# Last layer norm of tile 1's front half: moments turned into two rows and added by a rank-2 product, with GpSimd weighting by g and finishing one piece of tile 0

## The reference

```python
def layer_norm(x, g, b):
    xf = x.astype(jnp.float32)
    mu = jnp.mean(xf, axis=-1, keepdims=True)
    var = jnp.mean(jnp.square(xf - mu), axis=-1, keepdims=True)
    y = (xf - mu) * lax.rsqrt(var + LN_EPS) * g.astype(jnp.float32) + b.astype(jnp.float32)
    return y.astype(x.dtype)
...
        x = layer_norm(DEEPNORM_ALPHA * x + attn_out, ln1_g[l], ln1_b[l])
        hdn = jnp.square(jax.nn.relu(jnp.einsum('bsd,df->bsf', x, w_ff1[l])))
        ff_out = jnp.einsum('bsf,fd->bsd', hdn, w_ff2[l])
        x = layer_norm(DEEPNORM_ALPHA * x + ff_out, ln2_g[l], ln2_b[l])
```

## Time and profile before

| | |
|---|---|
| median of 3 runs | 1088.48 us (1087.71 to 1088.55) |
| the profiled execution | 1088.89 us, its span 1087.1 us |
| PE busy | 1081.4 us (99%) |
| DVE busy | 822.6 us (76%) |
| ACT busy | 578.2 us (53%) |
| POOL busy | 24.5 us (2%), 43 instructions |

### The profile page before, as it was taken

How to read it: one execution, slowest core, us unless ns; L and a number is a source line. 1 busy time by engine, 2 the same in 40 slices (tenths; PEclk the granted TensorE clock), 3 DMA queues, 4 the chain that set the end, 5 groups by cost and what they waited for, 6 DMA issues and landing times.

```text
span 1087.1 us, 13951 instructions
## 1 busy us (share of the span) xinstructions
PE 1081.4 (99%) x5586; PEld 918.4 (84%) x5586; DVE 822.6 (76%) x923; ACT 578.2 (53%) x756; POOL 24.5 (2%) x43
## 2 busy tenths in 40 slices
PE   9999999999999999999999999999999999999998
PEld 7888888888888888888888888888888888888886
DVE  6587758666666685667699999766776678889998
ACT  6487757665544524445465456444454455545461
POOL 1000101010000000000000000000000000000000
PEclk9999999999999999999999999999999999999999
DMA  9857665557545835665656566566656655655862
GB/s 300 263 177 224 185 191 156 175 177 247 176 155 168 285 108 156 192 193 176 218 189 231 169 220 232 167 188 191 191 174 204 219 177 198 228 195 190 282 222 78
DMA packets 108048, 213.84 MB, mean 197 GB/s; under 512 B 6784, under 2 KB 38016, under 8 KB 107472
## 3 DMA queue, kind: packets, MB, share of 16 engines
q1 hardware_dynamic: 107216, 209.61, 60.1%
q0 software_dynamic: 624, 3.21, 1.0%
q10 hardware_dynamic: 144, 0.13, 0.0%
HBM read 210.83 MB, written 2.10 MB: 196 GB/s over the span
## 4 chain that ended last, share of the span: by engine, by line
PE 98%; DVE 1%; DMA 1%; issue 0%; SPq 0%; ACT 0%; DVEq 0%
PE low_ps L802 11%; PE low_ps L639 10%; PE high_ps L802 9%; PE high_ps L824 7%; PE high_ps L823 7%; PE high_ps L822 7%; PE low_ps L531 6%; PE low_ps L527 6%; PE low_ps L529 6%; PE low_ps L808 5%; PE high_ps L808 5%; PE low_ps L644 5%; PE low_ps L823 3%; PE low_ps L824 3%; PE low_ps L822 3%; PE high_ps L576 1%
## 5 line engine op out<-in xcount | busy, mean ns | idle before, releaser
L1333 DVE TENSOR_TENSOR w_lo<-w_raw,w_hi 128x1024 fp32r<-128x1024 f32 x175 | 213.1, 1222 | 133.6 <-ACT w_hi L993 132.2
L993 ACT ACTIVATE w_hi<-w_raw 128x1024 fp32r<-128x1024 f32 x175 | 185.1, 1059 | 188.5 <-PE low_ps L531 69.5
L802 PE MATMUL low_ps<-x1T,w_hi 128*128 128x512 f32 x512 | 177.3, 393 | 0.0
L802 PE MATMUL high_ps<-x1T,w_hi 128*128 128x512 f32 x448 | 155.1, 393 | 0.0
L639 PE MATMUL low_ps<-xT,w_hi 128*128 128x512 f32 x448 | 144.2, 398 | 0.0
L808 PE MATMUL low_ps<-x1T,w_lo 128*128 128x256 f32 x512 | 139.3, 278 | 0.0
L1663 DVE TENSOR_TENSOR w_lo<-w_raw,w_hi 128x1024 fp32r<-128x1024 f32 x72 | 87.0, 1222 | 59.7 <-ACT w_hi L1194 59.7
L1218 ACT ACTIVATE sum_hi<-sum_raw 128x1024 fp32r<-128x1024 f32 x60 | 63.6, 1063 | 124.7 <-DVE sum_raw L1685 112.8
L808 PE MATMUL high_ps<-x1T,w_lo 128*128 128x256 f32 x448 | 122.1, 278 | 0.0
L1194 ACT ACTIVATE w_hi<-w_raw 128x1024 fp32r<-128x1024 f32 x72 | 76.1, 1060 | 86.4 <-PE low_ps L802 43.4
L802 PEld LDWEIGHTS low_ps<-x1T,w_hi 128*128 128x128 f32 x512 | 94.9, 187 | 20.1
(11 more groups left out here) (214 smaller groups left out, 1915.4 us busy)
## 6 DMA issues: line engine op xcount, KB each, us to landing
w_raw<-in_w_ff SPq DMA_DIRECT2D x208, 512.0 KB, 4.3
w_raw<-in_w_in SPq DMA_DIRECT2D x93, 512.0 KB, 4.3
more_raw<-in_w_ff SPq DMA_DIRECT2D x42, 512.0 KB, 5.2
w_raw<-in_w_out SPq DMA_DIRECT2D x32, 512.0 KB, 3.7
x_raw<-in_x_turned SPq DMA_DIRECT2D x8, 256.0 KB, 6.4
y<-in_x SPq DMA_DIRECT2D x8, 256.0 KB, 4.6
side_raw<-in_w_ff SPq DMA_DIRECT2D x4, 512.0 KB, 6.7
w_raw<-in_w_in SPq DMA_DIRECT2D x6, 256.0 KB, 5.8
```

Source lines behind the costliest of these rows:

```text
L802: return pe.matmul(banks[:, b, :], w_hi[:, slot, cols], x1T[:, t, :, :].rearrange("p h t -> p (h t)"), start=(t == 0 and not lows_open), s ...
L993: act.activation(w_hi[:, slot, :], w_raw[:, slot, :], ACT.Copy).then_inc(w_rounded, units)
L1333: dve.tensor_tensor(w_lo[:, slot, :], w_raw[:, slot, :], w_hi[:, slot, :].bitcast(F32), ALU.subtract).then_inc(w_split, units)
```

## The change

The moments of tile 1 no longer go through DVE's `centre` for its first half. With d the standard deviation and s = 1/d, the norm is written s(gy - mg + db). POOL multiplies the first half of tile 1 by g as soon as its four statistics are taken. PE brings this gy into PSUM through the identity. Once the moments are known, ACT takes the root d; PE turns the two columns (m, d) of 128 tokens into two rows of 128; ACT copies these out, with the sign of m flipped (`row_signs`); and PE adds for each piece one product of these two rows with two rows that hold g and b (`gb_rows`, loaded from HBM by two new DMAs of 4 KB). ACT's copy out of PSUM now multiplies by s. DVE's two `centre` instructions on this half are gone, and its four last instructions are two `centre` and two `finish_norm`.

Piece 2 of tile 0 leaves PE and ACT: POOL multiplies it by s and adds b, in two instructions. POOL thus runs three instructions on 1024, 512 and 512 columns that it didn't have. ACT runs one Sqrt ahead of the norm, and loads a table for it. DVE sets three small constants at the start. SP stores piece 3 ahead of piece 7.

```diff
 SCALED = [3, 4, 5, 6]
-COPIED = [2] + SCALED
-STORE_ORDER = [0, 1, 2, 7, 3, 4, 5, 8]
+FIRST_HALF = slice(0, HALF)
+BY_POOL = 2
+STORE_ORDER = [0, 1, BY_POOL, 3, 7, 4, 5, 8]
...
+                    sp.dma_start(gb_rows[n:n + 1, :], v[:, FIRST_HALF]).then_inc(rows_loaded, 16)
...
-        pe.wait_ge(tail_summed, 2)
-        pe.wait_ge(gb2_loaded, 32)
-        pe.matmul(high_ps[:, 1, :], ident_t[:, :], ln2_gb[:, 1, LAST_PIECES[2][1]], start=True, stop=False)
-        pe.wait_ge(diag_ready, 1)
-        pe.wait_ge(centred, len(PIECES) + 3)
-        pe.matmul(high_ps[:, 1, :], diag[0][:, :], y1[:, 0, LAST_PIECES[2][1]], start=False,
-                  stop=True).then_inc(y2_scaled, 1)
         pe.wait_ge(low_drained, 4)
+        pe.wait_ge(weighted, 1)
         for i in SCALED:
-            pe.matmul(scaled_ps(i), ident_t[:, :], ln2_gb[:, 1, LAST_PIECES[i][1]], start=True,
-                      stop=False)
-        pe.wait_ge(diag_ready, TT)
-        for n, i in enumerate(SCALED):
-            tt, cols = LAST_PIECES[i]
-            pe.wait_ge(centred, len(PIECES) + (6 if i > 4 else 4))
-            pe.matmul(scaled_ps(i), diag[1][:, :], y1[:, tt, cols], start=False,
+            pe.matmul(scaled_ps(i), ident_t[:, :], y1[:, 1, LAST_PIECES[i][1]], start=True, stop=False)
+        pe.wait_ge(tail_summed, 3)
+        pe.wait_ge(moments, 2 * TT)
+        pe.wait_ge(mean_std_ready, 1)
+        pe.matmul(high_ps[0:2, 2, 0:P], mean_std, ident_t[:, :], start=True, stop=True).then_inc(
+            moments_turned, 1)
+        pe.wait_ge(rows_loaded, 32)
+        pe.wait_ge(rows_ready, 1)
+        for i in SCALED:
+            pe.matmul(scaled_ps(i), moment_rows[0:2, :], gb_rows[0:2, LAST_PIECES[i][1]], start=False,
                       stop=True).then_inc(y2_scaled, 1)
...
-        def finish_piece(i, centred_before):
-            finish_norm(1, count + centred_before, 1, LAST_PIECES[i][1], y1, ln2_gb, y2_ready)
-
-        centre(1, 1, slice(0, 512), y1, ln2_gb)
         centre(1, 1, LAST_PIECES[7][1], y1, ln2_gb)
-        finish_piece(7, 5)
-        centre(1, 1, slice(512, 1024), y1, ln2_gb)
         centre(1, 1, LAST_PIECES[8][1], y1, ln2_gb)
-        finish_piece(8, 7)
+        finish_norm(1, count + 4, 1, LAST_PIECES[7][1], y1, ln2_gb, y2_ready)
+        finish_norm(1, count + 5, 1, LAST_PIECES[8][1], y1, ln2_gb, y2_ready)
...
+        pool.wait_ge(gb2_loaded, 32)
+        pool.wait_ge(y2_stats, 4)
+        pool.tensor_tensor(y1[:, 1, FIRST_HALF], y1[:, 1, FIRST_HALF], ln2_gb[:, 0, FIRST_HALF],
+                           ALU.mult).then_inc(weighted, 1)
+        inverse_std(1, 0)
+        front = y1[:, 0, LAST_PIECES[BY_POOL][1]]
+        pool.wait_ge(centred, len(PIECES) + 3)
+        pool.wait_ge(std_ready, TT + 1)
+        pool.tensor_scalar(front, front, inv_std[:, 0:1], None, ALU.mult).then_inc(front_scaled, 1)
+        pool.wait_ge(front_scaled, 1)
+        pool.tensor_tensor(front, front, ln2_gb[:, 1, LAST_PIECES[BY_POOL][1]], ALU.add).then_inc(
+            front_ready, 1)
+        inverse_std(1, 1)
```

More of the change, by code:

```diff
@@ L175, in hybrid_layer @@
     mid = at("mid", [P, 2 * TT, NC], F32, 48 * KB)
-    diag = [at(f"diag{tt}", [P, P], F32, 48 * KB + 512 * tt) for tt in range(TT)]
+    moment_rows = at("moment_rows", [P, P], F32, 48 * KB)
     X0 = 56 * KB
@@ L221, in hybrid_layer @@
     last_raw = at("last_raw", [P, 4 * NC], F32, H0 + 24 * KB)
+    gb_rows = at("gb_rows", [P, HALF], F32, X0 + 28 * KB)
     own_hi = [at("own_hi0", [P, 3 * NC], F32R, H0 + 77 * KB), at("own_hi1", [P, 3 * NC], F32R, X0)]
@@ L244, in hybrid_layer @@
     eps_sum = part(42, 2)
+    last_std, eps_one, row_signs = part(40, 1), part(44, 1), part(45, 1)
+    mean_std = small[:, 34:41:6]
     stats = part(48, TT * CHUNKS * 6 + 6)
@@ L313, in hybrid_layer @@
     y2_stats, y2_ready, stored = sem("y2_stats"), sem("y2_ready"), sem("stored")
-    diag_ready, y2_scaled, y2_copied = sem("diag_ready"), sem("y2_scaled"), sem("y2_copied")
+    rows_loaded, mean_std_ready, moments_turned = sem("rows_loaded"), sem("mean_std_ready"), sem("moments_turned")
+    rows_ready, y2_scaled, y2_copied = sem("rows_ready"), sem("y2_scaled"), sem("y2_copied")
+    weighted, front_scaled, front_ready = sem("weighted"), sem("front_scaled"), sem("front_ready")
     x_d = x.rearrange("b (t p) d -> p (b t) d", p=P)
@@ L452, in sync_program @@
             tt, cols = LAST_PIECES[i]
-            if i in COPIED:
-                sp.wait_ge(y2_copied, COPIED.index(i) + 1)
+            if i in SCALED:
+                sp.wait_ge(y2_copied, SCALED.index(i) + 1)
+            elif i == BY_POOL:
+                sp.wait_ge(front_ready, 1)
             else:
-                sp.wait_ge(y2_ready, i + 1 - len([n for n in COPIED if n < i]))
+                sp.wait_ge(y2_ready, [0, 1, 7, 8].index(i) + 1)
             sp.dma_start(out_d[:, tt, cols], y1[:, tt, cols]).then_inc(stored, 16)
@@ L1304, in scalar_program @@
         copy_first(3)
[L1306 to L1316, removed]
+        act.wait_ge(powers_ready, 5)
+        act.activation(last_std, eps_one, ACT.Sqrt)
+        act.wait_ge(moments, TT + 1)
+        act.activation(var_eps[:, 0:1], mean_var[:, 1:2], ACT.Copy, bias=EPS).then_inc(var_ready, 1)
+        act.wait_ge(moments, TT + 2)
+        act.activation(last_std, mean_var[:, 3:4], ACT.Sqrt, bias=eps_one).then_inc(mean_std_ready, 1)
+        act.activation(var_eps[:, 1:2], mean_var[:, 3:4], ACT.Copy, bias=EPS).then_inc(var_ready, 1)
+        act.wait_ge(moments_turned, 1)
+        act.activation(moment_rows[0:2, :], high_ps[0:2, 2, 0:P], ACT.Copy, scale=row_signs[0:2, :]).then_inc(
+            rows_ready, 1)
+        act.wait_ge(std_ready, 2 * TT)
         for n, i in enumerate(SCALED):
             tt, cols = LAST_PIECES[i]
-            act.wait_ge(y2_scaled, n + 2)
-            act.activation(y1[:, tt, cols], low_ps[:, n, 0:cols.stop - cols.start],
-                           ACT.Copy).then_inc(y2_copied, 1)
+            act.wait_ge(y2_scaled, n + 1)
+            act.activation(y1[:, tt, cols], low_ps[:, n, 0:cols.stop - cols.start], ACT.Copy,
+                           scale=inv_std[:, 1:2]).then_inc(y2_copied, 1)
         for i in BY_SCALAR:
             tt, cols = LAST_PIECES[i]
-            act.wait_ge(y2_copied, SCALED.index(i) + 2)
+            act.wait_ge(y2_copied, SCALED.index(i) + 1)
             act.dma_start(out_d[:, tt, cols], y1[:, tt, cols]).then_inc(stored, 16)
@@ L1449, in vector_program @@
         dve.memset(eps_sum, HEAD_DIM * EPS).then_inc(powers_ready, 1)
+        dve.memset(eps_one, EPS).then_inc(powers_ready, 1)
+        dve.memset(row_signs, 1.0).then_inc(powers_ready, 1)
+        dve.wait_ge(powers_ready, 4)
+        dve.memset(row_signs[0:1, :], -1.0).then_inc(powers_ready, 1)
         def split_opening(u):
@@ L1919, in rms_scale, with inverse_std, first_scale @@
             pool.tensor_tensor(o_scale, root, inv_sums[h % 3][:, 0:4:2], ALU.mult).then_inc(scale_ready, 1)
[L1921 to L1931, removed]
+        def inverse_std(norm, tt):
+            n = TT * norm + tt + 1
+            pool.wait_ge(var_ready, n)
+            pool.tensor_tensor(inv_std[:, tt:tt + 1], var_eps[:, tt:tt + 1],
+                               minus_half[:, tt:tt + 1], ALU.pow).then_inc(std_ready, 1)
+        def first_scale(tt):
+            pool.wait_ge(moments, tt + 1)
+            pool.tensor_scalar(var_eps[:, tt:tt + 1], mean_var[:, 2 * tt + 1:2 * tt + 2], EPS,
+                               None, ALU.add).then_inc(var_ready, 1)
+            inverse_std(0, tt)
         pool.wait_ge(w_used, SLOTS + 1)
@@ L1947, in gpsimd_program @@
                 "p l d -> p (l d)")).then_inc(gb1_loaded, 16)
-        norm_scale(0)
-        norm_scale(1)
+        for tt in range(TT):
+            first_scale(tt)
+        pool.wait_ge(gb2_loaded, 32)
[11 more added lines that the diff above has]
+        inverse_std(1, 1)
     with nc.Block() as block:
```

## The result

The changed kernel took 1090.8 us (median of 13 runs, 1089.98 to 1091.3), the kernel before 1088.28 in the same series (1087.71 to 1089.05). The ratio is 1.0022, with a 95% interval of 1.0015 to 1.0029: 2.4 us slower, between 1.6 and 3.2. The prediction was 1090.4, in a range of 1088.0 to 1091.2.

The account below looks back on a forecast made before the run. PE fills 98% of the chain, but DVE leads without a gap up to tile 1's moments. Terms 1.3 + 0.9 - 0.3 = +1.9 us, on the median of 1088.48, gave 1090.4 us, range 1088.0 to 1091.2.

Parts of the forecast that it names:

- What bounds it: DVE leads without a gap from tile 0's first block to tile 1's moments; before that its slack is 0.97 us.
- Start, table, small loads: Constants on DVE, ACT's table load and two 4 KB loads, all hidden in idle time or behind other work: 0.
- POOL's product by g: Before tile 0's first block: POOL streams 2.3 us and holds DVE, less 0.97 slack: +1.3.
- Piece 2 on POOL: End of tile 0's norm: POOL's add of b holds piece 0's `finish_norm`: +0.9, bounds 0 and 2.4.
- From T on: From the end of tile 1's moments (T) to the span's end: last store issued at T + 4.15, not T + 4.47: -0.3.
- My bound of 0: Smallest gain allowed after tile 1's moments, if the transfers themselves are the limit; the other bound was 0.6.
- The clock: Rival, 4%: PE waits about 2.2 us before the closing products, which run at 1.2 GHz; about 2.0 more, 1092.4.
- The sum: All terms together: 1.3 + 0.9 - 0.3 = +1.9 us.
- The rival in which DVE isn't held: POOL always gives way, so only the gain after tile 1's moments is left: 1088.2; 22%.
- the one in which POOL streams at half the rate: The product by g holds DVE 4.6 and PE starves; sum 5.7, 1094.2; 8%.
- Only one collision costs: Only the product by g (1089.5) or only piece 2's add (1089.1) holds DVE; 14%.

Follow-up runs that it names:

- both_retimed: The changed kernel with two more waits on POOL, moving its two two-input instructions to where DVE reads at most one SBUF input; +0.2 us against the kernel before.
- early_alone: The kernel before plus only POOL's product by g of 1024 columns, written to a tile that nothing reads; +0.9 us against the kernel before.
- early_one_input: The kernel before plus one POOL instruction with one input, adding a constant to 1024 columns that nothing reads; +0.1 us against the kernel before.
- retimed_reordered: The changed kernel with POOL's two two-input instructions delayed by waits, and SP's tile 1 stores ordered 7, 3, 8, 4, 5; -0.4 us against the kernel before.
- pe_filled: The changed kernel plus five PE products that nothing reads, four before the turning product and one behind it; +2.3 us against the kernel before.
- late_alone: The kernel before with only piece 2 of tile 0 finished by POOL instead of PE and ACT; +1.9 us against the kernel before.
- late_filled: The kernel before with piece 2 finished by POOL, plus five products that nothing reads in PE's wait before the closing products; +1.4 us against the kernel before.

## Why the prediction held, step by step

*What bounds it.* Right. DVE's 0.97 us was the room, and DVE led from `add_tail` to T: every held microsecond above 0.97 is in T.

*Start, table, small loads: 0.* No run singled these out, but the trace shows the table load (1.28) at 1061.95 in ACT's idle stretch. In both_retimed, which has all of them, DVE's stretch from `add_tail` to T has its old length.

*POOL's product by g: predicted 1.3, measured 1.03.* The mechanism, shown by early_alone and by both_retimed, is the one argued from rows that gave only its other half. The streaming was 2.26 where I had 2.3. The hold was 2.08, shorter than the streaming by 0.2, for which no row gives a reason; and another 0.1 came back in the four `w_lo` (4.62 for 4.74). The rule of the Trainium skill (SBUF — State Buffer, "Who interferes with whom") is borne out here for two inputs on both sides; by its letter the one-input instruction of early_one_input should have held DVE for its whole length, and the runs show 0.7.

*Piece 2 on POOL: predicted 0.9, measured 1.0, by the other of the two orders.* The scaling took 1.59, not 0.69, so that the add met `finish_norm` of piece 0 already running, waited for it, and held that of piece 1. The prediction had that case with 1.2; it is 1.02. The mis-sized term is the scaling; it happened to change little.

*From T on: predicted -0.3, measured +0.1.* This step failed. I had SP's five issues at 0.4 each, with the 0.43 of the row beside it; four of them take 0.43 to 0.46 and follow each other at 0.38 to 0.50. The first came 0.15 later than I had it (T + 2.65 for T + 2.5) and the four steps from there took 1.84 instead of 1.65, so that the last is issued at T + 4.49 and not T + 4.15. The rest is behind that issue: from it to the end of the span it is 3.04, where it was 2.96. I also treated the new order of stores as harmless. Piece 7 was ready at about T + 2.1 and waited behind piece 3 until T + 3.0. Another order of stores, and nothing else, moved the last issue from T + 4.50 to T + 4.03 and the end by 0.57 in the traces (7.54 in both_retimed, 6.97 in retimed_reordered). My bound of 0, "if the transfers themselves are the limit", isn't excluded: the DMA share is 0.97 and 1.05 in the two microseconds from 1085 on, and the last store took 2.6 to land where the other one of 256 KB took 2.2.

*The clock.* I gave the fall 4%; it fell. PE waited 2.27 and 0.54, near the 2.2 that I had, and the last closing products ran at 1.2 GHz. I priced it at 2.0; in the trace it costs 0.48 on ACT's branch and nothing at the end (pe_filled), because the stores end later. late_alone paid 1.1, since there the fall came earlier and all closing products ran at the lower clock. The trace doesn't speak for every timed run of the changed kernel. Its mean clock is 0.998, what a fall at 1083.7 gives; six of the thirteen runs have that and took 1089.98 to 1090.80. Four have 0.996, which takes a half clock for 7.6 us or more (an estimate from the mean), so from about T on, and they took 1091.07 to 1091.30. That the clock cost these four something is likely but not shown: pe_filled, at 0.998 or 0.999 throughout, also has three of its ten runs above 1091.1, and its median of 1090.57 is only 0.2 lower.

*The sum.* 1.9 predicted, 2.1 in the trace, 2.4 timed (1.6 to 3.2). Part of the closeness is luck: the product by g was 0.3 too dear, piece 2 0.1 and the stretch from T on 0.4 too cheap. Whether the last 0.3 of the time is real is not settled; it lies within the interval, and the runs with the early fall of the clock could be its source. The rival in which DVE isn't held is excluded by the rows, and so is the one in which POOL streams at half the rate. "Only one collision costs" is excluded too: each of the two, alone, makes its hold.

## What to carry to other kernels

A wide GpSimd instruction isn't free merely because GpSimd is idle. Look at what VectorE reads at that moment. Here a GpSimd instruction with two inputs cost nothing beside VectorE instructions with an input in PSUM, or statistics; in a closed run of two-input SBUF instructions it was paid for at nearly its full length (2.08 of 2.26 us), less the slack at VectorE's next wait. With one input it cost less (0.7) or nothing. Placing it is a matter of one semaphore.

When work is taken off TensorE near the end, the wait that it leaves can cost more than the work did; and when the last instructions on the data path get faster, check the stores behind them, their order first.

## What the hardware showed that I had not expected

- Two-input POOL instructions that nothing holds take 2.40 us for 1024 columns and 1.27 for 512 (both_retimed). A one-input one of 512 columns took 1.59 in all seven traces that have it, and one of 1024 took 3.62 in the place where the two-input one takes 3.24 (early_alone): slower with one input, not faster.
- The clock fell with PE's waits of 2.27 and 0.54 us between short groups of products (changed kernel, in the last closing products), with waits of only 0.23 and 0.54 (both_retimed, in the last closing products), and with one wait of 2.49 (late_alone, from the first closing product on). With waits of 0.22 and 0.54 in retimed_reordered it fell only behind the last product. In the traces of late_filled and pe_filled, where products that nothing reads filled the waits, it stayed at 1.00 to the last product. Kernels that differ only in POOL's or SP's timing, and runs of one kernel, thus fell at different moments.
- SP's DMA issues that follow one another without a pause take 0.43 to 0.46 us each in the changed kernel, the one after a wait 0.33.
